# Two transformer blocks in one kernel on Trainium2: the operands of the large matmuls at multiples of 512 bytes

## What is computed

```python
def first_block(x, c, ...):
    mod = silu(c) @ w_ada + b_ada                 # 2048 x 12288
    sh1, sc1, ga1, sh2, sc2, ga2 = split(mod, 6)
    h = modulate(rms_norm(x, g_norm1), sh1, sc1)
    qa, ka, va, oa, gates, qb, kb, vb = split(h @ w_in)      # 2048 x 7184
    h_a = mlstm_bidirectional(...)                # 4 heads of 256, gated by sigmoid(oa)
    h_b = neighborhood_attention(...)             # 8 heads of 128
    x = x + ga1 * (concat(h_a, h_b) @ w_out)      # 2048 x 2048
    h = modulate(rms_norm(x, g_norm2), sh2, sc2)
    u, g = split(h @ w_up)                        # 2048 x 11264
    x = x + ga2 * ((gelu(conv3(g)) * u) @ w_down) # 5632 x 2048
    return rms_norm(x, g_final)

def second_block(x, ...):
    h = rmsnorm(x, norm_mix_g)
    qa, ka, va, qb, kb, vb, ga, gb = split(h @ w_in)         # 2048 x 8704
    ya = sliding_window_attention(qa, ka, va, sinks) @ w_branch_a   # 1024 x 2048
    yb = stick_breaking_attention(qb, kb, vb) @ w_branch_b          # 1024 x 2048
    x = x + (sigmoid(ga) * ya + sigmoid(gb) * yb) @ w_out    # 2048 x 2048
    gate, up = split(rmsnorm(x, norm_ffn_g) @ w_ffn_in)      # 2048 x 11264
    x = x + (silu(gate) * up) @ w_ffn_down        # 5632 x 2048
    return rmsnorm(x, norm_final_g)
```

## The kernel before

| tile | first byte | mod 512 | mod 64 |
|---|---|---|---|
| `raw`, `w_hi`, `w_lo` | 16512, 32896, 49280 | 128 | 0 |
| `xres`, `h_hi`, `h_lo` | 65664, 82048, 98432 | 128 | 0 |
| `gate2`, `ident`, `ones`, `diag` | 114816 to 124032 | 128 | 0 |
| `c_act` (the last of `ctx`) | 128800 | 288 | 32 |
| `proj`, `a_hi`, `proj2`, `m_hi` | 128864 | 352 | 32 |
| `wg_hi`, `wg_lo` | 169824, 178016 | 352 | 32 |
| `m_lo`, `gates2`, `a_lo` | 145248, 165728, 173920 | 352 | 32 |
| `ada_sum`, `tmp`, `ada_ring`, `ff` | 186208, 198496, 210784, 218976 | 352 | 32 |
| `sink` | 229216 | 352 | 32 |

## Time and profile before

### The profile page before, as it was taken

How to read it: one execution, slowest core, us unless ns; L and a number is a source line. 1 busy time by engine, 2 the same in 40 slices (tenths; PEclk the granted TensorE clock), 3 DMA queues, 4 the chain that set the end, 5 groups by cost and what they waited for, 6 DMA issues and landing times.

```text
span 2826.4 us, 33726 instructions
## 1 busy us (share of the span) xinstructions
PE 2649.8 (94%) x11966; PEld 2154.5 (76%) x11966; DVE 1650.2 (58%) x1822; ACT 1203.0 (43%) x1516; POOL 130.9 (5%) x129
## 2 busy tenths in 40 slices
PE   0598998989999999999989999999999999999998
PEld 0577887778878787788878877777788888888886
DVE  7877674767767655644454465555555544454444
ACT  1143444434434343444444454554454454544333
POOL 2000002010000000000010030101000000000000
PEclk9999999999999999999999999999999999999999
DMA  9798776675767565555566644346466666665554
GB/s 384 272 331 286 242 261 177 199 241 194 244 201 244 186 198 158 192 186 185 167 194 193 192 120 142 104 145 213 156 185 187 191 186 191 188 187 189 189 187 142
DMA packets 273260, 567.38 MB, mean 201 GB/s; under 512 B 23957, under 2 KB 24301, under 8 KB 272653
## 3 DMA queue, kind: packets, MB, share of 16 engines
q1 hardware_dynamic: 272528, 565.78, 63.0%
q0 software_dynamic: 208, 0.18, 0.0%
q10 hardware_dynamic: 428, 0.14, 0.0%
HBM read 563.94 MB, written 2.10 MB: 200 GB/s over the span
## 4 chain that ended last, share of the span: by engine, by line
PE 82%; DMA 6%; DVE 6%; issue 2%; ACT 1%; SPq 1%; DVEq 0%; POOL 0%; POOLq 0%; ACTq 0%
PE gp L1125 25%; PE gp L1126 25%; PE gp L1127 25%; DMA ada_ring<-in_w_ada_dram 2%; DMA raw<-in_w_in_dram 2%; DMA proj<-in_w_ada_dram 2%; DVE ada_sum L1620 2%; DVE w_lo L1517 1%; ACT w_hi L683 1%; PE tp L1352 1%; PE tp L1394 1%; PE tp L1170 1%; SPq L444 0%; PE tp L1260 0%; PE tp L1161 0%
## 5 line engine op out<-in xcount | busy, mean ns | idle before, releaser
L1517 DVE TENSOR_TENSOR w_lo<-raw,w_hi 128x1024 fp32r<-128x1024 f32 x872 | 1068.5, 1230 | 920.1 <-ACT w_hi L683 915.0
L683 ACT CAST w_hi<-raw 128x1024 fp32r<-128x1024 f32 x872 | 910.9, 1050 | 1133.5 <-PE gp L1127 908.7
L1125 PE MATMUL gp<-w_hi,h_hi 128*128 128x512 f32 x2656 | 1051.5, 396 | 35.4 <-DVE w_lo L1517 31.5
L1127 PE MATMUL gp<-w_hi,h_lo 128*128 128x512 f32 x2656 | 1036.3, 390 | 0.0
L1126 PE MATMUL gp<-w_lo,h_hi 128*128 128x512 f32 x2656 | 1036.3, 390 | 0.0
L1125 PEld LDWEIGHTS gp<-w_hi,h_hi 128*128 128x128 f32 x2656 | 499.9, 188 | 155.3 <-DVE w_lo L1517 43.1
L1127 PEld LDWEIGHTS gp<-w_hi,h_lo 128*128 128x128 f32 x2656 | 499.6, 188 | 106.0
L1126 PEld LDWEIGHTS gp<-w_lo,h_hi 128*128 128x128 f32 x2656 | 500.1, 188 | 100.6 <-issue 0.2
L1125 PE MATMUL gp<-w_hi,a_hi 128*128 128x512 f32 x704 | 278.9, 396 | 0.0
L1126 PE MATMUL gp<-w_lo,a_hi 128*128 128x512 f32 x704 | 278.1, 395 | 0.0
L1127 PE MATMUL gp<-w_hi,a_lo 128*128 128x512 f32 x704 | 278.0, 395 | 0.0
(11 more groups left out here) (264 smaller groups left out, 1436.9 us busy)
## 6 DMA issues: line engine op xcount, KB each, us to landing
raw<-in_w_in_dram SPq DMA_DIRECT2D x248, 512.0 KB, 4.6
raw<-in_w_up_dram SPq DMA_DIRECT2D x176, 512.0 KB, 4.2
raw<-in_w_ffn_in_dram SPq DMA_DIRECT2D x176, 512.0 KB, 4.3
ada_ring<-in_w_ada_dram SPq DMA_DIRECT2D x128, 512.0 KB, 4.7
raw<-in_w_down_dram SPq DMA_DIRECT2D x88, 512.0 KB, 3.8
raw<-in_w_ffn_down_dram SPq DMA_DIRECT2D x88, 512.0 KB, 4.5
proj<-in_w_ada_dram SPq DMA_DIRECT2D x64, 512.0 KB, 8.7
raw<-in_w_out_dram SPq DMA_DIRECT2D x64, 512.0 KB, 4.6
```

Of the source, the lines that this page charges most:

```text
L683: nc.scalar.copy(w_hi[:, s], raw[:, s]).then_inc(hi_ready, 1)
L1125: mm(o, hi[:, kt0 + kt, ps], w_hi[:, s, k, :], start=n == 0, stop=False)
L1127: last = mm(o, lo[:, kt0 + kt, ps], w_hi[:, s, k, :], start=False, stop=n == g.kts - 1)
L1517: V.tensor_tensor(w_lo[:, s], raw[:, s], w_hi[:, s].bitcast(F32), ALU.subtract).then_inc(lo_ready, 1)
```

## The change

Two tiles that nothing reads or writes are added to `ctx`: `lead`, 96 words, ahead of `raw`, and `to_line`, 72 words, behind `c_act`. `tmp` has 192 words fewer. With the 384 bytes of `lead`, `raw` begins at 16896 = 33 × 512, and all tiles up to `diag` at a multiple of 512. `c_act` ends at 129248, and with the 288 bytes of `to_line` the stages' region begins at 129536 = 253 × 512. All tiles of the table except `c_act` and `sink` then have 0 in the third and the fourth column. The pieces of `tmp` begin at multiples of 128 words. Nothing else changes; the instructions are the same in number, order and size.

```diff
     with ctx:
 
+        sb("lead", [P, 96])
         raw = sb("raw", [P, RING, KB, CW])
         w_hi = sb("w_hi", [P, RING, KB, CW], F32R)
         w_lo = sb("w_lo", [P, RING, KB, CW], F32R)
@@ -172,6 +173,7 @@
         junk = sb("junk", [P, CW])
         mod = sb("mod", [P, 4, DT])
         c_act = sb("c_act", [P, DT])
+        sb("to_line", [P, 72])
         VC = {"c": 0, "g1": 16, "g2": 32, "mixg": 48, "ffng": 64, "ghead": 80, "gfin": 88}
@@ -239,7 +241,7 @@
         s3 = ExitStack()
         proj2 = sb("proj2", [P, ST, N_QKV2], scope=s3)
         gates2 = sb("gates2", [P, ST, 2 * D], scope=s3)
-        tmp = sb("tmp", [P, 7680], scope=s3)
+        tmp = sb("tmp", [P, 7488], scope=s3)
         sink = sb("sink", [P, HS], scope=s3)
```

## The result

The change takes the kernel from 2827.63 us to 2809.14 us (medians of four runs each), a ratio of 0.9934 with a 95% interval of 0.9922 to 0.9946. The forecast was 2810 us.

What follows compares the result with a forecast made beforehand. TensorE was taken to set the pace after a transfer-bound first 110 us; 2826.96 − 16.6 us from the a and m matmuls, all else 0, gave 2810 us (likeliest case 2804 to 2813), with a range of 2750 to 2830.

Steps and rivals of the forecast that it cites:

- (1): Left operands a and m, moved from 352 to 0: 2496 matmuls go from 233.3 to 226.7 ns, saving 16.6 us.
- (2): h and w matmuls, both operands moved from 128 to 0 with their distance kept: stay at 226.7 ns, no change.
- (3): Ten matmuls behind each transpose group in the h stages: start-up unchanged, taken as 0, bounds 0 to 4.3 us of gain.
- (4): VectorE and ScalarE work on the moved tiles: position costs VectorE nothing, and the same is taken for ScalarE.
- (5): Early transfers landing in `proj`, 16 to 107 us: taken as 0, between 2 us of gain and 2 of loss.
- Rival A: Whole kernel: nothing happens, the 233.3 ns of a and m has another source; 2827 us, chance 0.11.
- rival C: h matmuls rise to 233.3 ns, losing 43 us and up to 10 more, a and m gain nothing; 2870 to 2880, chance 0.12.
- Rival B: All large matmuls run at the full rate, 214.3 ns: 2682 to 2700 us, halfway 2755; chance 0.17, partway 0.09 of it.

Runs made afterwards that it cites:

- Only the stages' region: Changed kernel without `lead` and with `to_line` at 40 words, so proj, a, m, tmp at 0 mod 512, w, h, raw at 128; 2823.63 us, 0.9984 to before.
- Only the first piece: Changed kernel without `to_line`: w and h at 0 mod 512, a, m, proj and tmp at 224; 2826.36 us, ratio 0.9997 to the kernel before.

## Why the forecast held, point by point

(1) *a and m fall to h's interval, 16.6 us.* Right in size: 16.0 us by the three stages. Wrong in its reason. I saw 352 against 128 and named what the two tiles share (32 above a multiple of 64). The rows could not tell this from the distance to w, which also differed only in those two cases, 224 against 0. I had the distance under (2) as a possibility for h and did not carry it over to (1). The number survived by luck, because the change sets both right. With the reason that I gave, the kernel of "Only the stages' region" (a at 0, w at 128) would have been forecast some 14 us too fast in these three stages.

(2) *h stays.* Right, and for the reason that I had put second: w and h keep their distance. The sentence that the loss "grows with the columns" was wrong. The gates' 280 cycles are what 256 columns take at distance 224 (L115, (263.98 − 258.38) / 48 = 116.7 ns); at distance 0 they take 288, so this small product got slower by 48 × 3.3 ns = 0.16 us. For 256 columns zero is the slower distance. The fee at distance 0 is about 32 cycles for 256, 384 and 512 columns alike.

(3) *No change behind transposes.* Right in the sum, and wrong by its own sign. The ten matmuls that took 2.31 us in the earlier trace rows take 691.53 − 689.26 = 2.27 us in the changed kernel:

```profile
689.26 0.40 PE L1128 MATMUL gp<-w_lo,h_hi 128*128 128x512 f32 x1
...
691.53 0.39 PE L1129 MATMUL gp<-w_hi,h_lo 128*128 128x512 f32 x1
```

The next group behind transposes of `ff` goes the other way. The ten groups of `g_up` alternate between 2.31 and 2.29 us before, and between 2.28 and 2.31 in the change. Leaving out the kernel with h off by 32, both kernels with the region 224 from w alternate in the one way, and all five with it a multiple of 256 from w in the other; with the region 128 from w it is 2.28 and 2.29. So the start-up does depend on places. It is worth next to nothing: over the 45 groups of the h stages after 600 us whose ten intervals hold no wait, the mean of the ten matmuls is 2.298 us before and 2.295 after, 0.1 us in all.

(4) *VectorE and ScalarE.* Right: 1230 and 1229 ns, 1050 and 1051 on the two pages.

(5) *Transfers, taken as 0, at most 2 us.* Mis-sized: 2.3 to 3.4 us of gain, and the bound was too tight. The three profiles with the region off a multiple of 256 have the first large matmul at 113.8 to 114.2 us, the six with it on one at 110.4 to 111.5. I took the bound from the landing times of `ada_ring` and `raw`, both of which lay off a multiple of 256 (352 and 128). Two bad places next to each other say nothing about a good one.
The Trainium skill (DMA: Bandwidth & Descriptors, How a descriptor splits into AXI transactions) says of reading that a piece off a 256-byte boundary starts at the one below it, and nothing of landing. Carried over to landing, an estimate by its beats is 2.3% for the region 96 above a boundary, and 5.5% (135 beats for 128) for 224 above one. The trace has 2.7% for the first, 408 against 419 GB/s, but not more for the second, 410 GB/s in "Only the first piece", so it doesn't bear the count out as the cause.
The traces' records of single pieces of 4096 bytes say where the loss arises. From 16 to 95 us they take a mean of 163.2 ns before and 159.0 in the change. From 110 to 560 us, where they land in `ada_ring` and the DMA engines are less busy, the median is 159 ns in both, with `ada_ring` at 352 before. So the place costs where the transfers are the bound, and why it does stays open.

Rival A (nothing happens) and rival C (h loses its step) did not occur. C's price, put at 43 us and up to 10 more, was 39 in the kernel with h off by 32. Rival B, the full rate, is refuted further than by the result alone: at no distance did a group of 512 columns take less than 226.7 ns.

The parts add up to 16.0 + 2.3 to 3.4 = 18.3 to 19.4 us against 18.5 measured. The two profiled executions differ by more, 2826.4 − 2803.5 = 22.9 us. The 3 us beyond the parts lie between the first large matmul and the first of `g_up`: 527.0 us before, 524.3 and 523.9 in the two profiles of the change. The other kernels took 530.8, 528.2, 528.0, 524.8 and 527.2 us there (in the order of their experiments, without the one that slows h); the last three of them have `proj` at a multiple of 256. Whether a part of these 3 us belongs to the transfers that go on in that stretch, or all of it is scatter, stays open; the pieces' median of 159 ns in both kernels gives no sign of the transfers.

## What to carry to other kernels

In a stream of fp32r matmuls look at the start-to-start interval, and at the address of the left operand minus that of the right one, not at either alone: zero modulo 256 bytes is worth 6.7 ns of 233 here, with 512 right columns. With 384 a distance of 32 cost nothing, and with 256 zero was the slower one. Tiles that are allocated one after another slip off that by any small tile between them, so pad the small ones to 256 bytes; that also puts the landing places of a transfer-bound stretch where it moves 2.7% more. And when two positions differ in two ways at once, name both before one of them is put into the sum.

## What the hardware showed beyond that

- At distance 0 an fp32r matmul with 128 left columns costs 32 cycles above its right columns: 288, 417 and 544 cycles for 256, 384 and 512. With 64 left and 256 right columns it is 16. With 128 right columns it is 137.
- Away from 0, 512 columns cost 37 (distance 192) to 57 cycles (252) above, 48 at 32, 48, 64 and 224, and the intervals run in a fixed pattern of unequal ones, as 234, 231, 235, 233 ns with a before.
- With 384 columns a distance of 32 costs nothing (L117: (280.64 − 272.32) / 48 = 173.3 ns), and with 256 distances of 32 and 224 are even four and eight cycles ahead (L114 118.1 ns, L115 116.7, for 119.8 to 120.0 at 0). Of the widths tried, only the one of 512 loses by distance.
- Plain float32 matmuls, which take two cycles a column, show none of this at either place of that row, 224 and 0 from `ones`.
- Behind plain float32 work a chain at distance 0 takes 4 to 10 matmuls to settle at 226.7 ns, and where the tiles lie has a part in how many.
